# Delta rule: blocks of 32 inverted by two merges of four, in a longer fused kernel

## The reference

```python
def delta_rule_chunked(q, k, v, g, beta, s0):
    ...
    decay = jnp.exp(jnp.where(tril, gc[..., :, None] - gc[..., None, :], -jnp.inf))
    kb = kc * bc[..., None]
    vb = vc * bc[..., None]
    m = jnp.where(strict, jnp.einsum('bhncd,bhnsd->bhncs', kb, kc) * decay, 0.0)
    eye = jnp.eye(cl, dtype=f32)
    tmat = lax.linalg.triangular_solve(m + eye, jnp.broadcast_to(eye, m.shape), left_side=True,
                                      lower=True, unit_diagonal=True)
    u = jnp.einsum('bhncs,bhnsv->bhncv', tmat, vb)
    w = jnp.einsum('bhncs,bhnsk->bhnck', tmat, kb * jnp.exp(gc)[..., None])
    ...
    def step(s, inp):
        u_i, w_i, qk_i, qd_i, kd_i, gl_i = inp
        v_new = u_i - jnp.einsum('bhck,bhkv->bhcv', w_i, s)
        o_i = jnp.einsum('bhck,bhkv->bhcv', qd_i, s) + jnp.einsum('bhcs,bhsv->bhcv', qk_i, v_new)
        s = s * gl_i[..., None, None] + jnp.einsum('bhck,bhcv->bhkv', kd_i, v_new)
        return s, o_i
```

## Time and profile before

| | us |
|---|---|
| median of 3 runs | 3307.63 (3302.43 to 3307.97) |
| profiled execution | 3307.47 |
| its span in the trace | 3305.7 |
| TensorE busy | 3089.9 (93%) |
| VectorE busy | 1592.0 (48%) |
| ScalarE busy | 1207.9 (37%) |
| POOL busy | 289.7 (9%) |
| mean granted TensorE clock | 0.965 of full |

### The profile page before, as it was taken

One profiled execution on the slowest core, in us unless ns is written; L12 is line 12 of the kernel. 1 busy time (PEld: TensorE's weight loads), 2 busy tenths in 40 slices (PEclk: granted clock), 3 DMA queues, 4 the chain that ended last, 5 costly groups with the idle time before them and its releaser, 6 DMA issues.

```text
span 3305.7 us, 57546 instructions
## 1 busy us (share of the span) xinstructions
PE 3089.9 (93%) x24802; PEld 2456.4 (74%) x24802; DVE 1592.0 (48%) x2648; ACT 1207.9 (37%) x2206; POOL 289.7 (9%) x377
## 2 busy tenths in 40 slices
PE   7989998989999999889998899999999988999998
PEld 4767887757776787666775578888888866778886
DVE  3255445344525546645646555323235456653444
ACT  4315335355531654433324444111113434741221
POOL 1020020000002100133331000000000101000000
PEclk9999999989999999878999999999999989999999
DMA  6283213270227331322211004111212232032231
GB/s 216 77 326 110 102 59 103 102 255 27 84 99 256 106 108 51 111 72 68 99 45 42 27 14 102 64 64 51 77 51 76 76 65 64 8 96 93 86 115 64
DMA packets 175015, 306.83 MB, mean 93 GB/s; under 512 B 19270, under 2 KB 40583, under 8 KB 174505
## 3 DMA queue, kind: packets, MB, share of 16 engines
q1 hardware_dynamic: 147008, 278.81, 24.9%
q0 software_dynamic: 3712, 12.74, 1.4%
q10 hardware_dynamic: 24041, 11.60, 1.3%
HBM read 294.96 MB, written 6.80 MB: 91 GB/s over the span
## 4 chain that ended last, share of the span: by engine, by line
PE 72%; DVE 15%; ACT 8%; issue 2%; DMA 1%; POOL 1%; ACTq 0%; DVEq 0%; SPq 0%; POOLq 0%
PE psum L429 17%; PE psum L430 17%; PE psum L431 17%; PE psum L962 3%; PE psum L587 2%; PE psum L2504 2%; PE psum L981 2%; PE psum L2391 2%; ACT feat L696 2%; DVE weights_r L373 2%; DVE small L1126 2%; DVE arena L879 1%; PE psum L996 1%; DVE x_lat L882 1%; PE psum L2381 1%
## 5 line engine op out<-in xcount | busy, mean ns | idle before, releaser
L373 DVE TENSOR_TENSOR weights_r<-weights,weights_r 128x2048 fp32r<-128x2048 f32 (+1 forms) x166 | 361.3, 2196 | 496.9 <-ACT weights_r L364 496.6
L429 PE MATMUL psum<-feat_r,weights_r 128*128 128x512 f32 (+1 forms) x1536 | 537.7, 350 | 11.3 <-DVE feat_r L726 4.9
L429 PE MATMUL psum<-weights_r,feat_r 128*128 128x512 f32 (+2 forms) x1344 | 524.7, 390 | 13.0 <-DVE weights_r L373 9.1
L430 PE MATMUL psum<-feat_r,weights_r 128*128 128x512 f32 (+1 forms) x1536 | 535.4, 349 | 0.0
L431 PE MATMUL psum<-feat_r,weights_r 128*128 128x512 f32 (+1 forms) x1536 | 534.7, 348 | 0.0
L364 ACT ACTIVATE weights_r<-weights 128x2048 fp32r<-128x2048 f32 (+1 forms) x166 | 302.7, 1845 | 629.5 <-DMA weights<-in_w_ffn_gate 205.1
L431 PE MATMUL psum<-weights_r,feat_r 128*128 128x512 f32 (+2 forms) x1344 | 519.0, 386 | 0.0
L430 PE MATMUL psum<-weights_r,feat_r 128*128 128x512 f32 (+2 forms) x1344 | 518.6, 386 | 0.0
L429 PEld LDWEIGHTS psum<-feat_r,weights_r 128*128 128x128 f32 x1536 | 292.9, 191 | 55.7 <-issue 5.2
L431 PEld LDWEIGHTS psum<-feat_r,weights_r 128*128 128x128 f32 x1536 | 292.5, 190 | 36.6
L430 PEld LDWEIGHTS psum<-feat_r,weights_r 128*128 128x128 f32 x1536 | 292.9, 191 | 36.0
(11 more groups left out here) (482 smaller groups left out, 4230.2 us busy)
## 6 DMA issues: line engine op xcount, KB each, us to landing
weights<-in_w_mod SPq DMA_DIRECT2D x48, 2048.0 KB, 12.9
weights<-in_gla_w_in SPq DMA_DIRECT2D x24, 1024.0 KB, 7.3
weights<-in_w_ffn_gate SPq DMA_DIRECT2D x20, 1024.0 KB, 7.3
weights<-in_w_ffn_up SPq DMA_DIRECT2D x20, 1024.0 KB, 5.0
weights<-in_w_ffn_down SPq DMA_DIRECT2D x20, 1024.0 KB, 7.3
weights<-in_fox_w_in SPq DMA_DIRECT2D x16, 1024.0 KB, 7.1
weights<-in_sgu_w_in SPq DMA_DIRECT2D x12, 1024.0 KB, 6.3
weights<-in_gla_w_out SPq DMA_DIRECT2D x8, 1024.0 KB, 6.4
```

Source lines behind the costliest of these rows:

```text
L373: dve.e.tensor_tensor(WEI_r[:, s * SLOT:s * SLOT + n], WEI_t[:, s * SLOT:s * SLOT + n], WEI_r[:, s * SLOT + HALF:s * SLOT + HALF + n].bitc ...
L429: pe.e.matmul(ps, lh, rh, start=first, stop=False)
L430: pe.e.matmul(ps, lh, rl, start=False, stop=False)
```

## The change

A merge now takes four blocks into one, 2 to 8 and 8 to 32. With D the block diagonal, X its inverse, Y the transpose of X, and C the masked part between the blocks, E = X C has E to the fourth equal to zero, so the merged inverse is (I - E)(I + E E) X. `pe_et` makes the transpose of E, VectorE turns it (`dve_e`), `pe_e2` multiplies it by E and X side by side (64 columns, `PAIR`), which gives E E and E X; VectorE subtracts E X from X and transposes E E straight out of PSUM (`dve_g`), `pe_e2g` multiplies the two, and VectorE adds and transposes (`dve_x`). The constants for the stage are loaded over masks of an earlier stage when that is done.

```diff
+    STACK = own[4].rearrange("p (w h c) -> p w h c", w=4, h=8)
+    YS, XS = [STACK[:, 0], Y_ODD[:, :].rearrange("p (h c) -> p h c", h=8)], [STACK[:, 1], STACK[:, 3]]
+    ES, PAIR, ED_AT = STACK[:, 2], [STACK[:, 1:3], STACK[:, 2:4]], (0, 1)
...
+    def pe_e2(pe, n, m):
         for hb in range(2):
+            at = (D_, "e2", n, m, hb)
             ps = K.open(pe, at)
+            pe.wait_ge(*A.of((D_, "et", n, m, hb)))
+            pe.wait_ge(*V.of((D_, "e", n, m, hb)))
+            pe_strips(pe, by_heads(ps, 64), half(h8(VC), hb), PAIR[n % 2][:, :, 4 * hb:4 * hb + 4, :], at)
+
+    def pe_e2g(pe, n, m):
+        for hb in range(2):
+            at = (D_, "e2g", n, m, hb)
+            ps = K.open(pe, at)
+            pe.wait_ge(*V.of((D_, "e2t", n, m, hb)))
+            pe_strips(pe, by_heads(ps, 32), half(h8(VC), hb), half(XS[n % 2], hb), at)
...
-            pe_v(pe, n, 1)
-            pe_kq(pe, n, 1)
-            pe_z(pe, n, 1)
+            pe_et(pe, n, 0)
             if behind:
                 pe_join_v(pe, n - 1)
             pe_state(pe, n)
-            pe_v(pe, n, 2)
-            pe_warm(pe, spare)
+            pe_e2(pe, n, 0)
             if behind:
                 pe_join_z(pe, n - 1)
-            pe_z(pe, n, 2)
             if more:
                 pe_kq(pe, n + 1, 0)
-            pe_v(pe, n, 3)
-            pe_warm(pe, spare)
+            pe_e2g(pe, n, 0)
             if behind:
                 pe_cross(pe, n - 1)
-            pe_warm(pe, spare)
-            pe_z(pe, n, 3)
+            pe_et(pe, n, 1)
             if behind:
                 pe_corner(pe, n - 1)
-            pe_warm(pe, spare)
-            pe_v(pe, n, 4)
+            pe_kq(pe, n, 1)
+            pe_e2(pe, n, 1)
             if behind:
                 pe_u(pe, n - 1)
-            pe_z(pe, n, 4)
+            pe_e2g(pe, n, 1)
             if behind:
                 pe_s(pe, n - 1)
                 pe_o(pe, n - 1)
             pe_side(pe, gdn_side(n))
-            pe_warm(pe, spare, not gdn_side(n))
...
+    def dve_g(dve, n, m):
+        for hb in range(2):
+            at, X = (D_, "e2", n, m, hb), half(XS[n % 2], hb)
+            ps, w = by_heads(K.at[at], 64), ED_AT[n % 2]
             dve.wait_ge(*B.of(at))
             dve.chain()
+            dve.e.tensor_tensor(X, X, ps[:, :, 32 * w:32 * w + 32], ALU.subtract).then_inc(*V.put())
+            dve.e.transpose(half(h8(VC), hb), ps[:, :, 32 - 32 * w:64 - 32 * w]).then_inc(
+                *V.put(K.frees(V, at), (D_, "e2t", n, m, hb)))
...
-            dve_level(dve, n, 1)
+            dve_e(dve, n, 0)
+            dve_state(dve, n)
+            dve_g(dve, n, 0)
+            dve_x(dve, n, 0)
+            if more:
+                dve_kk(dve, n + 1, 0)
+                dve_kk(dve, n + 1, 1)
+            dve_e(dve, n, 1)
+            dve_g(dve, n, 1)
             dve_qk(dve, n)
-            dve_state(dve, n)
-            dve_level(dve, n, 2)
-            if more:
-                dve_kk(dve, n + 1)
-            dve_level(dve, n, 3)
-            dve_level(dve, n, 4)
+            dve_x(dve, n, 1)
...
+    def pool_masks(pool, n):
+        for m in range(2):
+            if n:
+                pool.wait_ge(*B.of((D_, "et", n - 1, m, 1)))
...
-    tiny_up = [m[:32, :32] for m in up[:5]]
+    tiny_up = [m[:32, :32] for m in (up[0], up[1] | up[2], up[3] | up[4])]
```

More of the change, by code:

```diff
@@ L2414, in pe_join_v @@
         for hb in range(2):
-            pe.wait_ge(*V.of((D_, "x level", n, 4, hb)))
+            pe.wait_ge(*V.of((D_, "y", n, 2, hb)))
         for h in range(8):
@@ L2426, in pe_join_z @@
         pe.wait_ge(*A.of((D_, "join v", n)))
-        for hb in range(2):
-            pe.wait_ge(*V.of((D_, "x turned", n, 4, hb)))
         for h in range(8):
-            x = XX[n % 2][:, 1, h, :]
+            x = XS[n % 2][:, h, :]
             for a in range(2):
@@ L2498, in pe_s @@
             done.then_inc(*B.put((D_, "s", n)))
-    def pe_warm(pe, ps, beside=True):
-        if beside:
-            pe.e.matmul(ps, ident, CONST[:, 0:NMAX], start=True, stop=True)
     def pe_gdn(pe):
@@ L2560, in act_gdn_begin @@
             act_to_tokens(act, ktok, (D_, "k"), m)
+        A.mark((D_, "key rows"))
     def act_decay_relu(act, n):
@@ L2735, in dve_first, with dve_e @@
         dve.chain()
-        dve.e.transpose(flat(Xt), flat(X)).then_inc(*V.put((D_, "x level", n, 0, 0), (D_, "x level", n, 0, 1)))
-    def dve_level(dve, n, level):
+        dve.e.transpose(flat(Y), flat(X)).then_inc(*V.put((D_, "y", n, 0, 0), (D_, "y", n, 0, 1)))
+    def dve_e(dve, n, m):
         for hb in range(2):
-            at = (D_, "z", n, level, hb)
-            Xt, X = (flat(XX[n % 2][:, w, 4 * hb:4 * hb + 4, :]) for w in range(2))
+            at = (D_, "et", n, m, hb)
+            dve.wait_ge(*A.of(at))
+            dve.e.transpose(flat(half(ES, hb)), VC[:, hb * 128:(hb + 1) * 128]).then_inc(*V.put((D_, "e", n, m, hb)))
@@ L2746, in dve_level, with dve_x @@
+    def dve_x(dve, n, m):
+        for hb in range(2):
+            at, X, Y = (D_, "e2g", n, m, hb), half(XS[n % 2], hb), half(YS[n % 2], hb)
+            dve.wait_ge(*B.of(at))
             dve.chain()
-            dve.e.transpose(X, Xt).then_inc(*V.put((D_, "x turned", n, level, hb)))
+            dve.e.tensor_tensor(flat(X), flat(X), K.at[at][:, 0:128], ALU.add).then_inc(*V.put(K.frees(V, at)))
+            dve.chain()
+            dve.e.transpose(flat(Y), flat(X)).then_inc(*V.put((D_, "y", n, m + 1, hb)))
@@ L2876, in pool_kd @@
                 pool.wait_ge(*B.of((D_, "s", n - 1)))
+            else:
+                pool.wait_ge(*A.of((D_, "key rows")))
             pool.e.tensor_tensor(grid(kd, 8), grid(ktok[:, t, :], 8), over(KD[:, t, d * 8:d * 8 + 8], 64),
```

123 lines of the change are left out of this document (51 added, 72 removed).

## The result

| | before | changed |
|---|---|---|
| median of 4 runs, us | 3305.03 (3300.3 to 3307.97) | 3247.49 (3243.34 to 3254.98) |
| ratio, 95% interval | | 0.983 (0.9807 to 0.9853) |
| span of the profiled execution, us | 3305.7 | 3244.1 |
| delta rule stage, us | 353.4 | 289.9 |
| mean granted clock in it | 0.886 | 0.818 |

The change saves 57.5 us where 17 were forecast, and 3247 lies outside the range of 3262 to 3326. The sign was right. Of the cases, rival 2 (3255) came nearest.

A forecast was written before the change was run, and what follows sets the result against it. It took TensorE, busy nearly without a break in the delta rule, as the bound. 54.4 us per pair against 58.2 gave -21 over 5.5 pairs, +5 first step and tail, -1 start: -17, so 3291 us, range 3262 to 3326.

The forecast's parts named there:

- rival 2: Delta rule stage: clock does as before, 12.3 low us a pair, 48.8 us per pair, 3255 us; chance 0.12.
- The price of a low microsecond, 0.38: Delta rule stage: each microsecond at 1.2 GHz costs 0.38 us, from a 42.3 us pair taking about 69 all low.
- The work at the upper clock: Delta rule stage: TensorE's work in a pair of steps takes 38.1 us at 2.4 GHz.
- The wide product: Merges of the inversion: a product with a 64-column right side takes 1.07 us, between 0.68 and 1.36.
- The waits behind other engines: TensorE in the delta rule: 2.7 + 0.8 + 0.7 = 4.2 us a pair, making 42.3 with the work.
- The bank of the second key products: Second pair of key products: TensorE waits 0.4 us in each step for VectorE to free the first pair's banks.
- The step-start wait: Start of the step after an even one: TensorE waits 2.7 us for E's first transpose behind VectorE's tail.
- it falls at that wait in each pair and returns only in the side product: Clock in the delta rule: low from the step's-start wait until the side product, 27 low us a pair.
- The ends: Outside the whole pairs: first step and tail +5 us without constants to hold the clock; program start -1.
- The instruction waits: TensorE in the delta rule: 20.9 us in twelve steps before, 1.7 a step, falling to 0.9 a step.
- Rival 1: Delta rule stage: clock stays low, 45 low us a pair, 61.2 us per pair, 3329 us; chance 0.20.
- Rival 3: VectorE's merge chain: reading every other 32 PSUM columns at twice 0.3 us eats the gain, 3306 us; chance 0.18.

The follow-up runs named there:

- a_narrow: The changed kernel with each wide product written as two narrow ones, 64 matmuls more a step; 3305.43 us.
- b_noconst: The kernel before without its matmuls of constants, nothing else changed; 3310.78 us.
- a_const: The changed kernel with matmuls of constants put back, five a step, four where the side product stands; 3257.83 us.
- a_narrow_const: The changed kernel with constants put back at five places a step and each wide product written as two narrow ones; 3319.30 us.
- s_turn_mid: The changed kernel with the side product halved over even and odd steps, and VectorE's next first transpose between decays' difference and clamp; 3233.06 us.
- a_query_first: The changed kernel with the second key/query product, and VectorE's part of it, back at the step's start; 3264.87 us.
- s_dif: The changed kernel with the side product halved over both steps and the decays' difference moved ahead of the second merge's subtract; 3253.78 us.
- the two second runs of the split kernels: Unaltered repeats of the changed kernel with the side product halved over both steps (3244.30 us), and of s_turn_mid (3236.22 us).

## Why the prediction was wrong

**The price of a low microsecond, 0.38, was right.** With it and the work at the upper clock, each stage closes. From before to changed: constants 55 x 1.05 = -58, products 0.6 x 12 = -7, issue waits -6.5, other waits +2, low time +25 x 0.38 = +9.5, sum -60 (measured -63.5). From changed to a_narrow: twice (1.36 - 1.03) x 12 = +8, issue +11, other -1, low +108 x 0.38 = +41, sum +59 (measured +63). From before to b_noconst: -58, issue +7, other -2, low +102 x 0.38 = +39, sum -14 (measured -14.4). From a_const to a_narrow_const: +8, +28, -3, +65 x 0.38 = +25, sum +58 (measured +58.3). From changed to s_turn_mid: -1.5, +1, -56 x 0.38 = -21, sum -22 (measured -19). These are sums over single executions and not proofs of each term, but in most no more than 4 us is missing; a_query_first, s_dif and the two second runs of the split kernels leave 5 to 7 open. There is a check that needs no sum. Within one kernel the work is the same, and executions differ in low time: over 161 executions, each against the mean of its kernel, one low us goes with 0.32 us of time. With the low time of all executions (45 to 54 more than before, not 25) the first sum above is about -50, and the eight executions of the changed kernel lie 51 under the kernel before.

**The work at the upper clock was right, its waits were too dear.** The wide product was taken at 1.07 and takes 1.03 to 1.10. The 0.68 that I had worked out from the Trainium skill (TensorEngine Tiling (Array Packing), Instruction Overhead) does not come out: the row at 1605.24 has 1.10. A pair's work of 38.1 us shows best in a_const, where most steps are at the upper clock and little waits: from the state product at 1423.84 to the second one after it at 1472.20 are 48.4 us at a clock of 1.00, less nine constants of 1.05 is 38.9. The waits behind other engines were put at 4.2 a pair. From 1401.9 to 1632.3, five pairs, the changed kernel's are:

```profile
PE psum L2392 <- DVE inverse_odd L2730: 2.6, 1, 2.6
...
PE psum L2392 <- DVE feat L2736: 1.8, 2, 1.2
PE psum L2382 <- DVE weights L2705: 1.0, 3, 0.4
PE psum L2382 <- DVE feat L2705: 0.6, 2, 0.4
```

That is 6.0 us, but the 2.6 end at 1402.06 and lie ahead of the five pairs; within them are 3.5, 0.7 a pair. The bank of the second key products is waited for in five of the ten steps, 0.4 us at most and 1.6 in all, where 0.4 in each was forecast. The step-start wait, 2.7 in every pair by my walk, comes twice in five pairs: where TensorE has just stood for instructions, as at 1591.68, VectorE has meanwhile caught up.

**The step that failed is "it falls at that wait in each pair and returns only in the side product", 27 low us a pair.** Measured over the same stretch: 230.4 us with 69 low (clock 0.85), 14 a pair. Both halves are wrong. The clock fell seven times in these five pairs, never at that wait and each time in an issue wait or within 2 us behind one. In the whole stage it fell about as often as before: 11 low stretches where before had 10, nine of the 11 within some 3 us of an issue wait. And it comes back after 10 us on average (109 / 11), without constants and ahead of the side product, as at 1601.8. The forecast read single low stretches and gave the constants the credit for their end. In b_noconst, low stretches last 18 us on average, up to 68. So without constants the clock stays low for long with the old products, and with the new ones it comes back all the same. With constants the new ones have four low stretches of 7 us on average (a_const).

So a pair takes 38.1 + 0.7 + 1.9 (issue waits) + 14 x 0.38 = 46.0, measured 46.1, where 54.4 was forecast: 4.9 of the 8.3 us are the low time, 3.5 the waits. Over five pairs that is 41 us of about 45 by which the profiled execution lies under the forecast.

**The ends were wrong by 6.** First step and tail were put at +5 for want of constants, beside half a pair's -1.9, so at +3. They took 62.6 us before and 59.5 after. The start was put at -1; the stage began 2.4 us later, and in the other traces of the changed kernel's variants between 1377 and 1389, so this is chance.

**The instruction waits were right in size and wrong in kind.** 0.9 us a step was taken, 9.5 us in ten steps measured. (The 20.9 before were the two largest rows; all rows give 23.3.) But they were treated as noise that shrinks a little. They stand where TensorE runs through its blocks fast, or where a load runs beside, and ahead of most of the clock's falls. Had I followed the 1644 matmul records that the stage would have fewer, I would have put low time down with them, and rival 2 would have had the larger chance.

**The rivals.** Rival 1 (clock stays low) did not come. Something like it happens with 64 matmuls a step more (a_narrow, clock 0.70, 3305), but behind issue waits (28.2 us, others 10.0), not behind VectorE as the rival had it. Rival 2 comes nearest, with 14 low us a pair where it had 12.3. That its 3255 was still 8 us too high is the waits: it kept the 4.2 a pair behind other engines, of which 0.7 came. Rival 3 is excluded by L2746 and L2747 at 0.29 and 0.31.

What stays open: why a low stretch ends when it does, and why it ends later with more narrow products. The traces show that it is so. Whether the clock in a_narrow stays low because of the waits or of the kind of work in between was not separated. Nor was it tested whether loads placed elsewhere would take issue waits away.

## What to carry to other kernels

Count TensorE's instructions and not only its microseconds: where many small matmuls follow one another, write two products with the same left side as one wide one, even if columns are computed that way at full price. Look for "issue" waits that cut a product in the middle, see whether a dense stretch or a load stands ahead of them, and try long matmuls with few instructions (here the side product, in halves) behind the dense parts. A filler matmul that holds the clock may be worth its time in one order and not in another, so it has to be tried again after each change of the work around it. And before an instruction is moved up to shorten a tail, look at when its load lands.

## What the runs showed of the hardware

- Instruction waits of TensorE lie at multiples of 254 records (381 + 380, 127 + 127, 1271 + 1270), and instruction packets have 16.4 KB. 768 matmuls more in the stage, all else equal, cost 48 to 58 us.
- At such a place TensorE waited in 81 of 177 cases when the DMA engines had been more than half busy for 4 us, in 118 of 294 when they had not and the last 254 records had passed in under 3.6 us, and in 15 of 650 otherwise.
- A constant of 128x512 every few us goes with 5.4 us of issue waits instead of 16.8, and with a clock of 0.96. It did so only for the new products; with the narrow ones 33.4 us remained.
- Of 156 waits of TensorE over 1 us that began at 2.4 GHz, 133 were followed by 1.2 GHz before 3 us had passed behind them, those for instructions (106 of 125) like those for other engines (27 of 31); of 184 waits of 0.3 to 1 us, 73. The level came back 3.4 to 17 us later in the changed kernel, and up to 68 later in b_noconst.
- A 32x64 product of 64 records takes 1.03 to 1.10 us where a 32x32 one takes 0.68; two narrow ones take 1.35.
- VectorE's subtract and transpose take 0.29 and 0.31 us, whether PSUM is read in one piece or every other 32 columns.
